# Branch gates computed with their weights stationary, and compressed scores woven into a merge-gate tile

## What is computed

```python
h = rms_norm(x, norm1_g)
proj = h @ w_in
(rx, rgate, q, kc, vc, ks, vs, kw, vw, nsa_g, mg_rnn, mg_attn) = jnp.split(proj, splits, axis=-1)
hr = rg_lru(causal_dwconv(rx, rnn_conv_w, rnn_conv_b), rg_w_a, rg_b_a, rg_w_x, rg_b_x, lru_lambda)
y_rnn = (hr * jax.nn.gelu(rgate)) @ w_rnn_out
o = nsa(q, kc, vc, ks, vs, kw, vw, nsa_g, ...)
y_attn = o @ w_attn_out
x = x + (jax.nn.sigmoid(mg_rnn) * y_rnn + jax.nn.sigmoid(mg_attn) * y_attn) @ w_out
```

```python
g = jax.nn.sigmoid(gates).reshape(bsz, s, N_KV, GROUP, 3).transpose(0, 2, 3, 1, 4)
sc = jnp.einsum('bgrqd,bgcd->bgrqc', qb, k_cmp).astype(f32) * scale
p_cmp = masked_softmax(sc, cmp_end[None, :] <= t[:, None])
```

## Time and profile before

| | us |
|---|---|
| median of 3 runs | 1190.6 |
| lowest and highest | 1188.79, 1192.44 |
| the profiled execution, its own time | 1188.86 |
| its span, as the trace counts it | 1187.1 |
| PE busy | 1152.3 |
| DVE busy | 903.9 |
| ACT busy | 684.9 |

### The profile page before, as it was taken

One profiled execution on the slowest core, in us unless ns is written; L12 is line 12 of the kernel. 1 busy time (PEld: TensorE's weight loads), 2 busy tenths in 40 slices (PEclk: granted clock), 3 DMA queues, 4 the chain that ended last, 5 costly groups with the idle time before them and its releaser, 6 DMA issues.

```text
span 1187.1 us, 25363 instructions
## 1 busy us (share of the span) xinstructions
PE 1152.3 (97%) x9641; PEld 1122.8 (95%) x9641; DVE 903.9 (76%) x1555; ACT 684.9 (58%) x1200; POOL 10.2 (1%) x13
## 2 busy tenths in 40 slices
PE   6999999999999999999999999999999999999996
PEld 6999999999899999999899899999998889999995
DVE  5788778667786998888777768777777766877775
ACT  6768764444465676556554456555565846555552
POOL 1000000000001000000000000000000000000000
PEclk9998999899999999999999999999999999999998
DMA  7665545422054676666553246666644423666660
GB/s 246 196 213 168 188 125 165 156 74 88 19 158 145 199 227 201 191 194 193 159 161 107 72 140 192 219 193 194 194 144 142 125 71 126 223 217 192 191 187 36
DMA packets 52779, 190.82 MB, mean 161 GB/s; under 512 B 5984, under 2 KB 5984, under 8 KB 52704
## 3 DMA queue, kind: packets, MB, share of 16 engines
q1 hardware_dynamic: 52416, 188.77, 50.9%
q10 hardware_dynamic: 288, 0.99, 0.2%
HBM read 188.69 MB, written 1.05 MB: 160 GB/s over the span
## 4 chain that ended last, share of the span: by engine, by line
PE 88%; DVE 5%; ACT 4%; issue 2%; DMA 1%; DVEq 0%; SPq 0%; ACTq 0%
PE bank L603 25%; PE bank L604 24%; PE bank L605 24%; PE bank L714 2%; PE bank L611 2%; PE bank L613 1%; PE bank L612 1%; DMA w_raw<-weight_stream 1%; DVE w_low L1644 1%; PE bank L725 1%; ACT w_high L1209 1%; PE bank L739 1%; PE bank L738 1%; PE bank L713 1%; PE bank L737 1%
## 5 line engine op out<-in xcount | busy, mean ns | idle before, releaser
L1644 DVE TENSOR_TENSOR w_low<-w_raw,w_high 128x1024 fp32r<-128x1024 f32 x356 | 434.4, 1223 | 147.1 <-ACT w_high L1209 144.9
L1209 ACT ACTIVATE w_high<-w_raw 128x1024 fp32r<-128x1024 f32 x356 | 375.3, 1058 | 268.9 <-PE bank L605 192.4
L603 PE MATMUL bank<-h_high,w_high 128*128 128x256 f32 x1760 | 495.4, 282 | 10.3 <-DVE h_low L1682 9.9
L604 PE MATMUL bank<-h_low,w_high 128*128 128x256 f32 x1760 | 488.8, 278 | 0.0
L605 PE MATMUL bank<-h_high,w_low 128*128 128x256 f32 x1760 | 488.6, 278 | 0.0
L603 PEld LDWEIGHTS bank<-h_high,w_high 128*128 128x128 f32 x1760 | 332.5, 189 | 12.0 <-issue 10.0
L604 PEld LDWEIGHTS bank<-h_low,w_high 128*128 128x128 f32 x1760 | 332.7, 189 | 0.4
L605 PEld LDWEIGHTS bank<-h_high,w_low 128*128 128x128 f32 x1760 | 332.7, 189 | 0.0
L603 PE MATMUL bank<-r_high,w_high 128*128 128x256 f32 x942 | 265.5, 282 | 3.9 <-ACT arena L1598 2.1
L604 PE MATMUL bank<-r_low,w_high 128*128 128x256 f32 x942 | 261.8, 278 | 0.0
L605 PE MATMUL bank<-r_high,w_low 128*128 128x256 f32 x942 | 261.7, 278 | 0.0
(11 more groups left out here) (207 smaller groups left out, 1159.0 us busy)
## 6 DMA issues: line engine op xcount, KB each, us to landing
w_raw<-weight_stream SPq DMA_DIRECT2D x356, 512.0 KB, 4.2
x<-x_in SPq DMA_DIRECT2D x4, 256.0 KB, 6.0
out<-arena SPq DMA_DIRECT2D x4, 256.0 KB, 2.3
small<-small_in ACTq DMA_DIRECT2D x1, 937.5 KB, 9.3
small<-small_in ACTq DMA_DIRECT2D x1, 30.5 KB, 3.8
```

The source lines that it names most:

```text
L603: mm(out_ap, wh, high, start=start, stop=False, skip_group_check=True)
L604: mm(out_ap, wh, low, start=False, stop=False, skip_group_check=True)
L1209: fn(w_high[:, c % RING, :], w_raw[:, c % RAW, :], ACT.Copy).then_inc(high_ready, 1)
L1644: v.tensor_tensor(w_low[:, c % RING, :], w_raw[:, c % RAW, :], f(w_high[:, c % RING, :]), ALU.subtract).then_inc(low_ready, 1)
```

## The change

It has two parts. In the first, the branch gates are computed with 48 weight columns stationary and 256 tokens moving: 24 matmuls of 256 columns, where 48 of 48 columns stood. The result has the gates on partitions and tokens along the row, so it has to be turned: ACT copies it to SBUF (`gates_copy`, after the high part of the last rx tile), PE turns it with two transposes after group t3, and ACT takes the two sigmoids after group t5. In the second, each pair of compressed score matmuls is followed by the three matmuls of one k of merge-gate tile 2, and the signal for the scores comes with the last one, just ahead of the last three matmuls of that tile.

```diff
@@ -881,10 +883,8 @@
             c = BASE["g"]
             chunk_here(c)
             for k in range(DT):
-                for t in range(TT):
-                    ins = moving_product(acc[2][:, t * 64:t * 64 + 3 * NH], c, k * P, 3 * NH,
-                                         h_high[:, k, t * P:(t + 1) * P], h_low[:, k, t * P:(t + 1) * P],
-                                         k == 0 and t == 0, k == DT - 1)
+                ins = split_product(acc[2][0:3 * NH, 0:S], c, k * P, h_high[:, k, :], h_low[:, k, :],
+                                    k == 0, k == DT - 1, width=3 * NH)
             ins.then_inc(chunk_used, 1)
@@ -900,6 +900,12 @@
                 if not ends_lru_chunk(t):
                     ins.then_inc(lru_done, 1)
+                if t == 3:
+                    pe.wait_ge(gates_copied, 1)
+                    for half in range(TT):
+                        ins = nc.tensor.transpose(acc[2][:, S + half * 64:S + half * 64 + 3 * NH],
+                                                  head_sq[0:3 * NH, 0, half * P:(half + 1) * P], ident[0:3 * NH, 0:3 * NH])
+                    ins.then_inc(gates_turned, 1)
@@ -977,16 +983,24 @@
-            for i in (1, 2):
-                pe.wait_ge(acc_read, 4 * ACC_YR + i)
-                merge_gates(i)
+            pe.wait_ge(acc_read, 4 * ACC_YR + 1)
+            merge_gates(1)
+            chunk_here(BASE["mg"] + 2)
+            pe.wait_ge(acc_read, 4 * ACC_YR + 2)
             pe.wait_ge(head_normed, 1 + 12)
             for t in range(TT):
                 for e in range(DT):
                     dst = bank[0][:, (t * NH + 2 * e) * 16:(t * NH + 2 * e + 2) * 16]
                     ins = mm(dst.rearrange("p (h c) -> p h c", h=2)[:, :, 0:NC], q0[:, e, t * P:(t + 1) * P],
                              cmp_k[:, :, e // 2:e // 2 + NKV * (NC - 1) + 1:NKV], start=True, stop=True)
-            ins.then_inc(cmp_scores, 1)
+                    n = t * DT + e
+                    if n == TT * DT - 1:
+                        ins.then_inc(cmp_scores, 1)
+                    if n % 2:
+                        k = n // 2
+                        ins = split_product(mg_bank(2), BASE["mg"] + 2, k * P, h_high[:, k, :], h_low[:, k, :],
+                                            k == 0, k == DT - 1)
+            ins.then_inc(chunk_used, 1)
@@ -1412,12 +1426,16 @@
+            def gates_copy():
+                act.wait_ge(chunk_used, BASE["g"] + 1)
+                fn(head_sq[0:3 * NH, 0, :], acc[2][0:3 * NH, 0:S], ACT.Copy).then_inc(gates_copied, 1)
+                split_high(BASE["g"] + RING)
+
             def branch_gates():
-                act.wait_ge(chunk_used, BASE["g"] + 1)
+                act.wait_ge(gates_turned, 1)
                 for t in range(TT):
-                    fn(stats[:, 200 + 48 * t:248 + 48 * t], acc[2][:, t * 64:t * 64 + 3 * NH],
+                    fn(stats[:, 200 + 48 * t:248 + 48 * t], acc[2][:, S + t * 64:S + t * 64 + 3 * NH],
                        ACT.Sigmoid, scale=rstd_col[:, t:t + 1]).then_inc(acc_read, 1)
-                split_high(BASE["g"] + RING)
@@ -1425,6 +1443,8 @@
                 if t == 1:
                     conv_high(RT - 1)
+                    gates_copy()
+                if t == 5:
                     branch_gates()
```

More of the change, by code:

```diff
@@ L352, in build @@
         head_normed = sem("head_normed")
+        gates_copied = sem("branch_gates_copied")
+        gates_turned = sem("branch_gates_turned")
         keys_spread = sem("branch_keys_in_other_half")
@@ L597, in _, with split_product @@
             mm = nc.tensor.matmul
-            def split_product(out_ap, c, col, high, low, start, stop):
-                wh = w_high[:, c % RING, col:col + P]
-                wl = w_low[:, c % RING, col:col + P]
+            def split_product(out_ap, c, col, high, low, start, stop, width=P):
+                wh = w_high[:, c % RING, col:col + width]
+                wl = w_low[:, c % RING, col:col + width]
                 mm(out_ap, wh, high, start=start, stop=False, skip_group_check=True)
```

## The result

| | before | after |
|---|---|---|
| median of 14 runs each | 1189.95 us | 1194.26 us |
| lowest and highest | 1186.64, 1193.08 | 1190.41, 1197.16 |
| ratio after to before | | 1.0035, 95% interval 1.0023 to 1.0047 |
| the profiled execution, its own time | 1188.86 us | 1190.41 us |
| its span | 1187.1 us | 1188.6 us |

The changed kernel is 4.2 us slower (0.35%). The forecast was 1192.4 us, +1.8, and "within 0.3%" as the likeliest; the time lies in the range of 1188.5 to 1196.5, but a little beyond the bound of 0.3%, which the interval of the ratio still takes in, and nearer to the first rival's +5.1 than to +1.8. The profiled execution of after is the lowest of its 14, so its trace shows the kernel at its best, and the difference of the two spans (1.5 us) is not the difference of the medians. Much of what follows turns on that.

What follows compares the result with a forecast made beforehand. It took PE, busy 97% of the 1187.1 us span, as the bound. 1188.86 + 2.1 (gates) - 0.3 (scores) = 1190.7 for the profiled execution, 1192.4 us on the median; range 1188.5 to 1196.5, its own 1191.7 to 1193.6.

Steps and rivals of the forecast that it cites:

- within 0.3%: Whole kernel: too little change to tell from none, 3.6 us either way, 1187.0 to 1194.2 us; chance 0.55.
- first rival: Tile 5's wait: old kernel often holds its clock at the scores, so the new order costs +3.0, in all +5.1; chance 0.36.
- PE's wait for the copy: Gates, after t3: PE idle from 102.2 to 107.5 until ACT's copy; t4 starts at about 107.9, 0.7 us later.
- The clock behind the idle time: Groups t4 to t7: PE restarts at 1.2 GHz for 2.9 to 5.9 us; t8 starts between 112.1 and 113.3.
- Nothing behind t8 takes the loss back: After the gates: the +2.1 us loss stays whole, since PE sets the pace there.
- The woven tile's own cost: Merge-gate tile 2 with the scores: 0.86 us a pair, eight pairs 6.96 us, ending at 221.4, clock held.
- T + 8.6: Start of tile 5, 8.6 us after tile 2 ends (T = 221.4), so 230.0 against 230.29 before; PE idle 2.2 us.
- part two: Compressed scores woven into merge-gate tile 2: worth -0.3 us, bounds -0.4 and +0.3.
- The drop inside the woven part: Woven tile 2: the clock falls there too, tile 5 at 231.0 to 231.6, total 1193.4 to 1194.0 us; chance 0.07.
- The free case: Gates: part one costs nothing, as full clock returns at once or PE catches up behind ACT; 1190.3 us; chance 0.10.
- the gain of 7.2 us: Gates: the apparent gain of 7.2 us arrives, with 2.5 at the scores; 1180.9 us; chance 0.05.
- part one: Branch gates on PE: costs 1.5 to 2.7 us, middle +2.1, through the copy wait and half clock.

Runs made afterwards that it cites:

- second repeat of before: The unedited kernel before, profiled a third time for its trace; 1190.49 us.
- late copy: Four traces of kernels with ACT's copy of the gates placed as in after, behind the high part of the last rx tile; after itself measured 1194.26 us.
- scores alone: Before with only the scores woven into merge-gate tile 2, gates as they were; 1192.04 us, ratio to before 1.0015.
- scores alone first: Before with the woven scores, and DVE's mask, maximum and subtraction moved ahead of tile 2's scaling and split; 1189.68 us, ratio to before 0.9991.
- first repeat of before: The unedited kernel before, profiled a second time for its trace; 1191.42 us.
- gates filled: Before with only the changed gates, plus 44 unused products of 256 columns on PE ahead of the wait for the copy; 1193.09 us, ratio to before 1.0026.
- both repaired: After with ACT's gate copy moved earlier and DVE's score steps ahead of tile 2's scaling; run twice: 1188.51 us, ratio to before 0.9979, and 1190.51 us, 0.9999.
- repeat of after: The unedited kernel after, profiled a second time for its trace; 1195.61 us.

## Why the prediction was right and wrong

**PE's wait for the copy: right, by its mechanism.** It said t3 near 101.5, idle until 107.5 with ACT's copy as releaser, two transposes in 0.3, t4 at 107.9. The trace has 101.86, 107.76, 0.38 and 108.14, of which 0.35 is the later position of the whole. The copy took 0.36 us on a forecast of 0.4. The pair of transposes took 0.38 us at half clock, where 2 x 275 ns from the Trainium skill, "TensorE: Matmul & The Clock Gate", section "PE-mode transpose", would have been 0.55. But that was a wrong use of the figure, not a wrong figure. The view by line of before, with the mean duration of one in ns, has the eight 128 x 128 transposes ahead of tile 5 at 272:

```profile
L996 PE MATMUL bank<-small,arena 128*128 128x128 f32 x8 | 1.0, 272 | 0.0
```

So one lasts as long as the page says, and yet the next starts 0.105 us after it. Their durations overlap and don't add.

**The clock behind the idle time: right.** It restarted at half clock and took until 111.5, which is 3.4 us and inside the 2.9 to 5.9 us taken from the earlier trace rows. t8 came 2.0 us later on a forecast of 2.1. The price of a slow product, 0.213 us, is right too, though "25.7 of them" is not a count: from 101.95 to 107.43 there are 25 starts and 0.15 us extra behind the first product.

**"Nothing behind t8 takes the loss back": wrong.** A grew by 1.3, not 2.0. Between 112 and 214 PE waits for ACT behind the lru stage. Here is that view, of the second repeat of before and then of after:

```profile
PE bank L914 <- ACT arena L1433: 2.1, 2, 1.4
```

```profile
PE bank L920 <- ACT arena L1453: 0.8, 1, 0.8
```

There are up to two such waits. The later one takes 0.7 or 0.8 us in every trace. The earlier one stands in three of the five traces with the old gates, 0.23 us in before (PE's timeline) and up to 1.45, and in none of the four with the late copy:

```profile
125.42 0.61 PE L914 MATMUL bank<-small,arena 128*128 128x2 f32 x4 [0.23 <-ACT arena L1433]
```

In sum the waits are 1.0, 0.8, 2.1, 1.6 and 0.7 us with the old gates (before, its repeats, scores alone, scores alone first) and 0.8, 0.8, 0.7 and 0.7 with the late copy. Taken out of A, they leave 106.7 to 107.0 with the old gates and 108.5 to 108.8 with the late: the loss of +1.8 stands in every trace, and on the mean 0.5 us of it is given back, since a late PE finds ACT ready. In the first repeat of before and in scores alone first, where the earlier wait is missing, nothing would be given back. So what is given back is worth about 0.5 us and shows in three of five traces; the other 0.2 between t8 and tile 2 stays open. The wait was in the trace of before, and the prediction didn't look for it: "PE sets the pace there" gives no row.

**The woven tile's own cost: right in kind, too high in size.** The clock held in all eight woven tiles, and tile 5 came at T + 8.67 behind a wait of 2.19 us, on a forecast of T + 8.6 and 2.2. The pair was 0.80 us, not 0.86: the four passes cost 0.09 each instead of 0.107 (0.36 from 216.44 to 216.80), the first long product behind them 0.20, the two others 0.12 each. So against the trace part two was worth 15.88 - 15.07 = -0.8, not -0.3. That is outside the bounds of -0.4 and +0.3, which by the forecast's own terms should have read about -0.5 and +0.1. The steps were sound, and the gain against this one trace was larger than forecast.

**What part two was compared with: wrong.** The sum took 15.88 as what the old scores cost. That was the dearest of the executions seen; three of six hold the clock and need 12.9, and the mean is 13.88. That is the first rival's mechanism. It named 227.0 for tile 5 with the clock held, 12.6 behind tile 2, and 12.87 was found; its condition, that more than about half of the executions hold it, came out at just three of six, and where it holds, the woven order costs +2.2, so the mechanism is worth +1.2 on the mean and not its whole +3.0. The forecast should have used a mean over both cases here, because both occur among six traces of the same order, while the prediction treated the rival as a case that is either true or false. Its price of +3.0 was too high for a mixture; whether 0.36 was too low, one outcome can't say.

**What stands behind tile 5: missing.** The prediction knew a restart at half clock after 9.08 us of idle time and took one after 5.3, but priced PE's new 2.2 us of idle time by its length alone. In three of four traces the clock falls within the first 1.0 us of tile 5 (at once, after 0.5 and after 1.0 us), for 3.3 to 3.5 us, at 1.5 us each; in the ten traces without this wait it never falls there. This is +1.1 that no term and no rival held. Without it the sum would be +2.5, inside the forecast's own range (+1.1 to +3.0, or 1191.7 to 1193.6); with it and what is left open the time lies above.

**The other rivals.** The drop inside the woven part came in none of eight. The free case and the gain of 7.2 us were not seen: PE's 7.6 us less of busy time went into 4.9, 2.2 and 2.0 us of waits, as the rows of the waits view show.

In sum, +2.1 - 0.3 = +1.8 should have been +1.3 + 1.2 + 1.1 = +3.6, and that the time lies in the wide range of 1188.5 to 1196.5 is partly luck: its upper end was set by a rival's price, and not by the piece that was missing. The first two errors (0.8 too much in part one, 1.5 too little in part two) cancel in part, the third is whole.

## What to carry to other kernels

Short products that let the clock fall are cheap to remove only if the engine isn't idle afterwards: if PE now waits for a copy or a scaling on another engine, the clock can fall again right behind the wait, so first move that step to the head of its queue (here 3.4 us for one move on DVE). And ask whether the slow stretch costs anything where it stands: at the old gates 10.3 or 6.8 us of it gave the same start of t8, since PE otherwise waited for ACT. A trace is one draw: when a price rests on whether the clock fell, profile the old kernel three times or more and use the mean of what it did, and look where the profiled time lies among the runs. A loss ahead of a stage in which the bounding engine already waits a little for somebody can be partly given back there.

## What the runs showed of the hardware

- The same kernel on the same data loses its clock or keeps it behind the same 32 short passes: 6.8, 3.4 and 0 us at 1.2 GHz in three executions. At the 48 products of 48 columns the same three spent 10.3, 6.8 and 6.8 us there.
- 2.2 us without work in front of tile 5, amid streaming products, were followed by a fall to 1.2 GHz in three of four executions, and the ten without this wait have none there. About 2.0 us without work ahead of t3 were followed by a fall in some traces and not in others: t3's first product takes 0.58 us in gates filled, and 0.38 in after.
- Short fp32 passes of 30 columns between long products cost 0.09 us each, and 0.109 in a row of 32 (3.49 us); a product of 256 columns costs 0.113, hardly more.
- In three of fourteen executions products near the kernel's start take twice as long, though the window shows a granted clock of 1.00. Here is that stretch in before, with 29 products, and in both repaired, with 18:

```profile
14.50:18.40 3.90, 3.73 (x29) 3.62 (x30) 3.83 (x6) 3.20 (x7) 0.00 (x0) 1.00 0.45 134
```

```profile
14.50:18.40 3.90, 3.86 (x18) 3.86 (x19) 3.83 (x5) 3.49 (x7) 0.00 (x0) 1.00 0.41 112
```

- It came with old and new gates alike (scores alone first, the repeat of after, both repaired), so it is spread and no effect of the change, and its cause was not looked for. In these three ACT's last high part of rx starts at 109.0 to 109.6, in the others at 106.7 to 108.0. A milder case lies at 346 to 366, where PE gets through 179 products in before and 172 in its first repeat, also at a clock of 1.00. These are two of the places in which executions of one kernel differ; the fourteen of before lie within 6.4 us, those of after within 6.8.
